# Scaling the attention probabilities on GpSimd in a two-block network on one core

## What is computed

```
s = jnp.einsum('bqhd,bkhd->bhqk', qi, k).astype(jnp.float32) * scale
s = jnp.where(mask[None, None], s, NEG_INF_2)
p = jax.nn.softmax(s, axis=-1).astype(v.dtype)
return jnp.einsum('bhqk,bkhd->bqhd', p, v)
```

## Time and profile before

| | us |
|---|---|
| device time, median of 3 runs | 2902.02 |
| lowest and highest | 2899.57, 2903.31 |
| span of the profiled execution, first to last instruction | 2897.1 |
| PE busy in it | 2493.3 (86%) |
| DVE busy | 1267.2 (44%) |
| ACT busy | 980.2 (34%) |
| POOL busy | 743.6 (26%) |

### The profile page before, as it was taken

One profiled execution on the slowest core, in us unless ns is written; L12 is line 12 of the kernel. 1 busy time (PEld: TensorE's weight loads), 2 busy tenths in 40 slices (PEclk: granted clock), 3 DMA queues, 4 the chain that ended last, 5 costly groups with the idle time before them and its releaser, 6 DMA issues. The chain is left out here.

```text
span 2897.1 us, 34583 instructions
## 1 busy us (share of the span) xinstructions
PE 2493.3 (86%) x13054; PEld 1942.8 (67%) x13054; DVE 1267.2 (44%) x2608; ACT 980.2 (34%) x1580; POOL 743.6 (26%) x204
## 2 busy tenths in 40 slices
PE   6988888787993887999899388979999889989998
PEld 4756777666772575667677265858887746668886
DVE  3554555446445414784555545143222463243123
ACT  2432111224552112772445224152323433343222
POOL 2430000032342230001343220313443202324441
PEclk9998899988996896999899698999999999999999
DMA  4342000016883233111788331313322302223321
GB/s 108 90 148 105 1 1 1 30 45 219 278 284 138 77 103 128 44 35 45 241 284 283 109 91 44 96 58 105 126 91 79 106 23 65 81 84 105 106 80 66
DMA packets 228189, 304.46 MB, mean 105 GB/s; under 512 B 52320, under 2 KB 139888, under 8 KB 228032
## 3 DMA queue, kind: packets, MB, share of 16 engines
q1 hardware_dynamic: 225744, 294.16, 31.5%
q0 software_dynamic: 2304, 8.39, 0.8%
HBM read 270.95 MB, written 31.56 MB: 104 GB/s over the span
## 5 line engine op out<-in xcount | busy, mean ns | idle before, releaser
L159 POOL TENSOR_TENSOR branch_weights_wl<-branch_weights_wf,branch_weights_wh 128x2048 fp32r<-128x2048 f32 (+1 forms) x66 | 303.9, 4604 | 767.5 <-ACT branch_weights_wh L153 767.5
L153 ACT ACTIVATE branch_weights_wh<-branch_weights_wf 128x2048 fp32r<-128x2048 f32 (+1 forms) x66 | 125.0, 1895 | 404.1 <-PE bprojc_acc L201 132.0
L201 PE MATMUL merge_acc<-xh,branch_weights_wh 128*128 128x512 f32 x384 | 151.5, 395 | 2.9 <-PEq L72 2.9
L201 PE MATMUL merge_acc<-xh,branch_weights_wl 128*128 128x512 f32 x384 | 150.6, 392 | 0.0
L201 PE MATMUL merge_acc<-xl,branch_weights_wh 128*128 128x512 f32 x384 | 149.6, 390 | 0.0
L159 POOL TENSOR_TENSOR nsa_weights_wl<-nsa_weights_wf,nsa_weights_wh 128x2048 fp32r<-128x2048 f32 x13 | 59.8, 4601 | 279.8 <-ACT nsa_weights_wh L153 279.8
L1606 PE MATMUL exp_ps_y<-rt_wf,exp_ht 128*128 128x512 f32 x256 | 118.9, 608 | 3.8 <-ACT exp_ht L1650 3.8
L159 POOL TENSOR_TENSOR in_weights_wl<-in_weights_wf,in_weights_wh 128x2048 fp32r<-128x2048 f32 x16 | 75.2, 4701 | 158.3 <-ACT in_weights_wh L153 140.2
L1460 POOL TENSOR_TENSOR rt_wl<-rt_wf,rt_wh 128x2048 fp32r<-128x2048 f32 x16 | 82.6, 5162 | 129.0 <-ACT rt_wh L1456 129.0
L201 PE MATMUL gproj_acc<-xh,in_weights_wh 128*128 128x512 f32 x256 | 103.0, 402 | 2.5 <-POOL in_weights_wl L159 2.5
L201 PE MATMUL gproj_acc<-xl,in_weights_wh 128*128 128x512 f32 x256 | 101.0, 394 | 0.0
(11 more groups left out here) (614 smaller groups left out, 6680.9 us busy)
## 6 DMA issues: line engine op xcount, KB each, us to landing
branch_weights_wf<-w_in SPq DMA_DIRECT2D x56, 1024.0 KB, 5.0
rt_wf<-moe_w_down SPq DMA_DIRECT2D x32, 1024.0 KB, 5.4
in_weights_wf<-gdn_w_in SPq DMA_DIRECT2D x16, 1024.0 KB, 5.5
rt_wf<-moe_w_gate SPq DMA_DIRECT2D x32, 512.0 KB, 7.2
rt_wf<-moe_w_up SPq DMA_DIRECT2D x32, 512.0 KB, 8.1
moe_rows<-rt_y SPq DMA_DIRECT2D x64, 256.0 KB, 2.1
moe_rows<-gproj_zeros SPq DMA_DIRECT2D x2, 6144.0 KB, 27.9
merge_bwf<-w_branch SPq DMA_DIRECT2D x12, 1024.0 KB, 5.0
```

The source lines that it names most:

```text
L153: act.activation(self.h[u][:, :, 0:self.cols(b)], self.s.f[u][:, :, 0:self.cols(b)], ACT.Copy).then_inc(self.s.hi_ready, 1)
L159: pool.tensor_tensor(self.l[u][:, :, 0:self.cols(b)], self.s.f[u][:, :, 0:self.cols(b)], self.h[u][:, :, 0:self.cols(b)].bitcast(F32), ALU ...
L201: mm = pe.matmul(self.acc[:, s, 0:cols], lhs[:, P * s:P * s + P], rhs, start=(u == 0 and k == 0 and n == 0), stop=(u == 1 and k == HALF - ...
```

## The change

The two scaling instructions of each unit go from DVE's list to POOL's, as the method `pool`, with the same operands. POOL waits until the reciprocal (in `natt` the product with the gate) is done, which the counter `r_step` tells, and raises `normed`, for which PE's turn waits as before. DVE no longer waits for its own last step. In `batt` the masks come in pieces: the first four before everything, the two of each later pair between the scalings of the pair before, each ahead of a scaling.

```diff
-    def mask_diagonals(self, pool):
-        pool.wait_ge(self.m_loaded, 16)
-        for h in range(self.heads):
-            pool.wait_ge(self.b_loaded[h % 4], 16 * (h // 4 + 1))
-            diag = self.bt[h % 4][:, 0:P]
-            pool.tensor_tensor(diag, diag, self.mt[:], ALU.add).then_inc(self.masked, 1)
+    def mask_diagonal(self, pool, h):
+        if h == 0:
+            pool.wait_ge(self.m_loaded, 16)
+        pool.wait_ge(self.b_loaded[h % 4], 16 * (h // 4 + 1))
+        diag = self.bt[h % 4][:, 0:P]
+        pool.tensor_tensor(diag, diag, self.mt[:], ALU.add).then_inc(self.masked, 1)
...
+    def pool(self, pool, u):
+        width = self.unit(u)[3]
+        pool.wait_ge(self.r_step, (2 if self.gate else 1) * (u + 1))
+        for e in range(2):
+            ins = pool.tensor_scalar(self.s[u % 3][:, e, 0:width], self.s[u % 3][:, e, 0:width],
+                                     self.r[u % 3][:, e:e + 1], None, ALU.mult)
+        ins.then_inc(self.normed, 1)
...
             dve.reciprocal(self.r[u % 3][:], self.l[u % 3][:]).then_inc(self.r_step, 1)
-            steps = 2 if self.gate else 1
-            dve.wait_ge(self.r_step, steps * u + 1)
             if self.gate:
+                dve.wait_ge(self.r_step, 2 * u + 1)
                 dve.tensor_tensor(self.r[u % 3][:], self.r[u % 3][:], self.gate(hp, i, b), ALU.mult).then_inc(self.r_step, 1)
-                dve.wait_ge(self.r_step, steps * u + 2)
-            for e in range(2):
-                ins = dve.tensor_scalar(self.s[u % 3][:, e, 0:width], self.s[u % 3][:, e, 0:width],
-                                        self.r[u % 3][:, e:e + 1], None, ALU.mult)
-            ins.then_inc(self.normed, 1)
...
                 if mask is not None:
-                    at.mask_diagonals(pool)
+                    for h in range(4):
+                        at.mask_diagonal(pool, h)
+                for u in range(at.U):
+                    if mask is not None and u >= at.pair_units and u % at.pair_units < 2 and u // at.pair_units + 1 < heads // 2:
+                        at.mask_diagonal(pool, 2 * (u // at.pair_units + 1) + u % at.pair_units)
+                    at.pool(pool, u)
```

## The result

| | before | changed |
|---|---|---|
| device time, median of 4 runs each, us | 2902.66 | 2974.25 |
| lowest and highest | 2899.57, 2907.45 | 2973.52, 2975.42 |
| span of the profiled execution | 2897.1 | 2971.7 |

The ratio is 1.0242, 95% interval 1.0228 to 1.0256: the changed kernel is 2.4% slower, 71.6 us by the medians. The sign was forecast, the size was not: 2919.5 was said, and 2952 was the end of the range.

What follows compares the result with a forecast made beforehand. PE was taken to bound `natt` (146 of about 158 us), with the scaling itself on the path at two places per pair. `natt` +14.6 and the other four stages +2.9 made +17.5 us, 2919.5; range 2897 to 2952.

Steps and rivals of the forecast that it cites:

- The price on POOL: Each moved scaling instruction: midway between MEMSET and TENSOR_TENSOR, 1.02 us at 512 columns and 0.79 at 384, two per unit.
- `natt`, first units: First 512-wide unit of each pair +1.16 us, first 384-wide +0.67 after 0.16 slack; eight pairs, +14.6 us.
- `natt`, second units: Second units of both widths in each pair wait for the later PE anyway and cost nothing.
- Three stages taken from one: One `matt` or `batt` stage was read, +0.73 us, and the other three taken as equal: +2.9 us.
- The gap at a pair's end: In `matt` and `batt` the output's multiplication starts 0.63 us earlier, shrinking three gaps per stage, -1.89 us each stage.
- Rival (c): POOL scales at TENSOR_TENSOR's price in all stages: +59 us, 2961, with a lower PE clock besides; chance 0.20.
- GpSimd's idle stretch: In `natt`, POOL was busy for none of about 158 us before the change.
- the ISA instructions ahead of the first scaling: One ISA instruction before POOL's first scaling, taken as 0, at most 6.5 us, once.
- the bias additions: DVE's bias additions, with one operand in PSUM, overlap POOL's instructions without getting longer; counted as nothing.
- masks that never hold a scaling: In `batt` the masks share POOL's queue, but their waits and 0.46 us of work hide in an idle stretch: 0.
- VectorE's subtraction in `matt`: Behind the gap in `matt` and `batt` it can wait some 0.5 us for POOL's second instruction, at cost 0.
- VectorE's gate multiplication: In `natt` the gate's 128x2 multiplication runs before POOL gets its unit, so the two do not exclude each other.

Runs made afterwards that it cites:

- e1: Changed kernel with POOL scaling only as many columns of each unit as cost the forecast's prices, the rest left unscaled; 2918.33 us.
- e11: Changed kernel with the second 512- and 384-wide unit of each `natt` pair scaled in all but their last 180 columns; 2996.32 us.
- e10_before_fill: Kernel before, with 12 identity transposes in TensorE's 2.02 us wait before the first 512-wide turn of later `matt` and `batt` pairs; 2896.61 us.
- e5_fill: Changed kernel, with TensorE's wait before each pair's first 512-wide turn filled by identity transposes (16 in `natt`, 12 elsewhere); 2957.86 us.
- e4_order: Kernel before, scaling still on DVE, with the output's multiplication issued ahead of the scaling where a `matt` or `batt` pair ends; 2892.29 us.
- e6: Changed kernel, but VectorE scales head 0 of each unit and GpSimd head 1, TensorE waiting for both; 2919.33 us.
- e3: Changed kernel with the scaling on POOL only in the four `matt` and `batt` stages, on DVE in `natt`; 2933.16 us.

## Why the prediction came out as it did

**The price on POOL** is the step of the prediction that failed: 1.02 and 0.79 us were taken for 512 and 384 columns, and 1.56 and 1.24 were measured. At the price that was taken the same code came out at 2918.3 us (e1). Halfway between MEMSET and TENSOR_TENSOR was reasoned from the number of tensors read. The row that was called the upper bound was none: a TENSOR_SCALAR costs 0.28 us before its first column, a TENSOR_TENSOR about 0.10 (457 - 128 x 2.76), and per column they differ little (2.5 and 2.76 ns). What one read less saves, the instruction's start takes back. "GPSIMD Engine Reference" of the Trainium skill, section 4.1, calls operations of one input roughly line-rate; the trace disagrees, with 1562 ns on GpSimd and 440 on VectorE for the same instruction.

**`natt`, first units.** The mechanism held. With the measured prices the forecast's formula gives 8 x ((3.12 - 0.88) + (2.49 - 0.75 - 0.16)) = 30.6 us, and at the forecast's own price it was met (e1).

**The handover** was missing: 0.10 us on GpSimd, where VectorE had 0.04 between its own instructions; 0.06 more at each of 16 places, 1.0 us.

**`natt`, second units.** "Cost nothing" was right at 1.02 us (in e1 the second turns come no later in six of eight pairs) and wrong at 1.56, since GpSimd then needs 3.1 us for a unit and TensorE less: 3 to 4.5 us (e11). A condition stood in the forecast's sentence ("POOL is free again after 2.04 while a wide unit takes over 2"), and it wasn't carried to the rival with the higher price. Turn by turn, from e10_before_fill to e5_fill, a pair grows by 4.3 us: 2.29 at the first 512-wide turn, 0.79 and 0.83 at the second 512-wide and first 384-wide ones (together about the 1.64 that the formula and the handover give for the chain through ACT), and 0.40 at the second 384-wide one. The formula's 3.82 with both handovers is 3.94. 30.6 + 1.0 + 4 = 36, against 192.8 - 155.8 = 36.9 with the clock held up.

**Three stages taken from one.** At the measured price the formula gives each stage 2.24 + 3 x 0.41 + 3 x 1.18 + 1.56 = 8.6 us. From e10_before_fill to e5_fill the `batt` stages grew by 8.5 and 7.7 us and the `matt` stages by 3.5 and 4.1. That the first agrees is luck: in `batt` the first pair cost 3.7 to 4.5 us and not 2.24, since its 256-wide unit, the first of the stage, had no slack either, and the 384-wide turns behind the gaps cost 0.76 (1.13 in the last pair) and not 1.18 (1.56). One reason for the lower cost in `matt` stands in the trace of before:

```profile
1771.65 0.75 DVE L2220 TENSOR_SCALAR matt_s<-matt_s,matt_r 128x384 f32<-128x384 f32 x2
...
1771.95 1.98 PE L2131 MATMUL matt_pss<-br_mk,br_mq 96*128 96x512 f32 x4
...
1773.77 0.49 PE L2142 MATMUL matt_pst<-ident,matt_s 128*128 128x128 f32 x3
```

In `matt` TensorE's scores of the next unit take 1.98 us (1.13 in `batt` for the same 512 columns, by the run e4_order), so the 384-wide turn has 1773.77 - 1772.40 - 0.06 = 1.31 us of slack, and not the 0.56 of `batt`. It was to be read in the rows of before. By that 0.43 of the 2.49 - 0.75 = 1.74 us would be left at each of these turns, but e5_fill shows nothing left:

```profile
1811.48 1.09 PE L2150 MATMUL matt_pst<-ident,matt_s 128*128 128x128 f32 x8 [0.62 <-POOL matt_s L2181]
1811.61 0.17 DVE L2229 RECIPROCAL matt_r<-matt_l 128x2 f32<-128x2 f32 x1
1811.87 2.47 POOL L2181 TENSOR_SCALAR matt_s<-matt_s,matt_r 128x384 f32<-128x384 f32 x2 [0.44 <-DVE matt_r L2229]
...
1814.91 0.82 PE L2150 MATMUL matt_pst<-ident,matt_s 128*128 128x128 f32 x6
```

The 384-wide turn still comes 0.57 after its scaling (1814.91 - 1814.34). The forecast took its slack as fixed, and it is not. Before, ACT was late in the gap and released the 512-wide turn, and the reciprocal of the 384-wide unit ended 1.25 us after that turn began. Now GpSimd is late, ACT goes on beside it, and that reciprocal ends 0.29 after the turn in `matt` and 0.79 in `batt`. So a `matt` stage paid 0.45 at each of its three gaps, 0.63 at the last 384-wide turn, and the rest at its first units.

**The gap at a pair's end.** That the multiplication is late behind the scaling was right (e4: 5.7 us in the four stages). But the changed kernel could take the gain only if GpSimd ended by 1915.74, and at 3.1 us it didn't: the turn then waits for GpSimd (at 2.04 us it did, e1). In `batt` the multiplication also started no earlier, since the turn ahead of it waited 0.53 us for GpSimd.

**Rival (c)** was the one that came: TENSOR_TENSOR's price, with the clock. Its 59 us are close to the 60.7 of the stages with the clock held up, though by errors that cancel (the second units left out, the `matt` stages too dear). The clock came on top, some 11 us. It had a chance of 0.20, and the range ended at 2952, below the 2961 that the rival gives even without the clock.

**Right as said:** GpSimd's idle stretch and the order of the change; the ISA instructions ahead of the first scaling, 10 ns each; the bias additions, no longer than before; masks that never hold a scaling; VectorE's subtraction in `matt`, held for 0.47 us where some 0.5 was said, at no cost. **Wrong without weight:** VectorE's gate multiplication does meet GpSimd (last section).

## What to carry to other kernels

Moving work to an idle engine is free only where the moved step has at least as much slack as it grows by; count the slack unit by unit, since here half of the steps moved for next to nothing and the other half cost nearly everything. Count it again for the new kernel: when another engine becomes the late one, the slacks behind it change. A price that no row shows should be bounded by the start of an instruction as well as by its slope, and where the candidates differ threefold the range has to hold the dearest one with all that follows from it, the slower clock too. And look first for the gain in the order of the old engine's list: that alone took some 6 us out of the four stages, where the move cost 71.6.

## What the runs showed of the hardware

- A tensor_scalar with a value per partition on GpSimd, 32-bit: 331, 562, 792, 1022, 1243 and 1562 ns for 20, 112, 204, 296, 384 and 512 columns; beside VectorE's scaling of the other head 1471 ns at 384 and 1858 at 512.
- GpSimd beside an earlier VectorE scaling of the other head (e6): it lost the time beside each other less 0.13 us, at all four widths (0.30, 0.23, 0.16 and 0.10 us).
- VectorE beside an earlier GpSimd scaling: the gate's multiplication of two small SBUF tensors took 0.60 us instead of 0.16 where it started 0.09 us into GpSimd's instruction (1239.71 and seven more), and `matt`'s subtraction of two SBUF tensors 1.16 instead of 0.69 where it started 0.06 in (six). Both were let through some 0.53 us after GpSimd's start, with 1 us of its 512-wide instruction still to run. Starting 0.46 us or more into it, the same multiplication (seven) and `batt`'s subtraction (six) took their usual 0.16 and 0.69; one that started 0.34 in took 0.26. The bias additions kept their 0.69. Nothing was seen to wait for the delayed ones.
- TensorE's granted clock fell from 0.98 to 0.91 in `natt` when one wait per pair grew from 0.35 to 2.62 us; the same instructions took 9% longer there (146.15 to 159.12), and filling that wait brought `natt` back to 0.98. In the shorter stages the clock of one and the same code differs between executions: `batt0` had 0.76 in the changed kernel (26% longer, 33.96 to 42.90) and 0.82 in e3.
